# Expert blocks of 96 rows instead of 128, a shorter routing list, score products issued in pairs

## The reference

```
n = rmsnorm(x);  z = n @ w_in            # 1024 -> 3072: q, k, v, and B, C, h of the convolution
o = rmsnorm(diff_attention(q, k, v))     # 4 heads, two softmax maps each, relative-position bias
c = rmsnorm(B * causal_conv(C * h))      # width 3
h = x + concat(o, c) @ w_out
m = rmsnorm(h)
group = argmax(m @ router_group)         # 4 groups of 8 experts
top 2 of the group's 8 experts, gates from two softmaxes
y = h + sum over the token's 2 experts e of gate[e] * (silu(m @ w_gate[e]) * (m @ w_up[e])) @ w_down[e]
out = rmsnorm(y)
```

## Time and profile before

| what | value |
|---|---|
| median of three runs | 1072.74 us (1069.87 to 1073.26) |
| the profiled execution | 1070.95 us, its span 1069.1 us |
| TensorE busy | 916.2 us (86%) |
| VectorE busy | 577.2 us (54%) |
| ScalarE busy | 499.4 us (47%) |
| GpSimd busy | 442.3 us (41%) |
| moved over the span | 206.25 MB, mean 193 GB/s |

### The profile page before, as it was taken

The page is one execution under the profiler, slowest core; times in us unless marked ns, Lnnn a source line. Parts: engine busy times, 40 slices in busy tenths (PEclk is TensorE's granted clock), DMA queues, the critical chain, the costliest instruction groups (busy, mean ns, idle before and its releaser), DMA issues.

```text
span 1069.1 us, 14098 instructions
## 1 busy us (share of the span) xinstructions
PE 916.2 (86%) x4937; PEld 749.7 (70%) x4937; DVE 577.2 (54%) x1032; ACT 499.4 (47%) x830; POOL 442.3 (41%) x332
## 2 busy tenths in 40 slices
PE   4899999999999999958969997289999999999700
PEld 3799887888788778845757665178888887777500
DVE  4504532353325332767645137787777767767347
ACT  4423344334433434253312121558888877777412
POOL 1102322222332323223313120078999975565475
PEclk9999999999999999979979998589999999999955
DMA  8033223232121103270253521989999999998785
GB/s 263 18 93 101 80 80 94 88 99 80 41 62 30 51 28 103 86 236 1 83 168 119 177 84 64 360 311 376 410 412 406 413 405 399 402 397 329 280 283 204
DMA packets 92554, 206.25 MB, mean 193 GB/s; under 512 B 12767, under 2 KB 54303, under 8 KB 84294
## 3 DMA queue, kind: packets, MB, share of 16 engines
q1 hardware_dynamic: 79950, 168.13, 43.3%
q10 hardware_dynamic: 5528, 20.04, 4.8%
q0 software_dynamic: 7008, 17.18, 4.5%
HBM read 171.19 MB, written 42.34 MB: 200 GB/s over the span
## 4 chain that ended last, share of the span: by engine, by line
PE 66%; DVE 10%; DMA 9%; issue 5%; POOL 4%; ACT 4%; SPq 2%; ACTq 0%; POOLq 0%; DVEq 0%
PE pj L971 25%; PE pj L1854 11%; PE pj L1060 7%; DMA e_raw<-in_w_up 7%; PE pj L1900 6%; PE pj L1037 5%; PE pj L1022 3%; POOL f_y L2112 2%; PE tp L1829 2%; PE tp L1011 1%; DVE e_lo L1806 1%; DVE sc L1253 1%; DMA k_page<-in_cache_k 1%; PE pj L1452 1%; PE tp L994 1%
## 5 line engine op out<-in xcount | busy, mean ns | idle before, releaser
L971 PE MATMUL pj<-n_hi,w_hi 128*128 128x350 f32 (+1 forms) x576 | 200.3, 348 | 3.4 <-DVE n_lo L1291 3.4
L1806 POOL TENSOR_TENSOR e_lo<-e_raw,e_hid 128x2048 fp32r<-128x2048 f32 x32 | 167.6, 5237 | 72.8 <-ACT e_hid L1802 72.7
L971 PE MATMUL pj<-n_lo,w_hi 128*128 128x350 f32 (+1 forms) x576 | 188.4, 327 | 0.0
L971 PE MATMUL pj<-n_hi,w_lo 128*128 128x350 f32 (+1 forms) x576 | 187.5, 325 | 0.0
L1806 DVE TENSOR_TENSOR e_lo<-e_raw,e_hig 128x2048 fp32r<-128x2048 f32 x64 | 148.6, 2324 | 0.1
L669 POOL TENSOR_TENSOR w_lo<-w_raw,w_hi 128x1024 fp32r<-128x1024 f32 x21 | 50.1, 2388 | 204.5 <-ACT w_hi L744 204.5
L1802 ACT ACTIVATE e_hig<-e_raw 128x2048 fp32r<-128x2048 f32 x64 | 122.7, 1919 | 25.3 <-DMA e_raw<-in_w_up 18.7
L971 PEld LDWEIGHTS pj<-n_hi,w_hi 128*128 128x128 f32 x576 | 109.7, 190 | 32.3 <-issue 30.4
L1253 DVE CUSTOM_DVE_ANT_0 sc<-pj,strip 128x512 f32<-128x512 f32 (+5 forms) x120 | 61.6, 545 | 102.1 <-PE pj L1037 60.6
L971 PEld LDWEIGHTS pj<-n_lo,w_hi 128*128 128x128 f32 x576 | 110.0, 191 | 0.6
L971 PEld LDWEIGHTS pj<-n_hi,w_lo 128*128 128x128 f32 x576 | 109.8, 191 | 0.7 <-issue 0.6
(11 more groups left out here) (257 smaller groups left out, 1710.8 us busy)
## 6 DMA issues: line engine op xcount, KB each, us to landing
e_raw<-in_w_up SPq DMA_DIRECT2D x32, 1024.0 KB, 18.3
e_raw<-in_w_gate SPq DMA_DIRECT2D x32, 1024.0 KB, 20.4
e_raw<-in_w_down SPq DMA_DIRECT2D x32, 1024.0 KB, 21.9
expert_rows<-yo ACTq DMA_DIRECT2D x32, 512.0 KB, 8.2
w_raw<-in_w_in SPq DMA_DIRECT2D x24, 512.0 KB, 3.9
expert_rows<-logits SPq DMA_DIRECT2D x16, 512.0 KB, 5.1
wo_raw<-in_w_out SPq DMA_DIRECT2D x8, 512.0 KB, 5.0
k_page<-in_cache_k SPq DMA_DIRECT2D x16, 256.0 KB, 3.8
```

Source lines behind the costliest of these rows:

```text
L971: ins = pe.matmul(pj[g % 2][:, 0:tn], ws[w][:, P * k:P * (k + 1)], x[:, k, t0:t0 + tn], start=(m == 0), stop=(m == 23))
L1806: eng.tensor_tensor(e_lo[r][:, q, :], e_raw[r][:, q, :], e_hi(par, q).bitcast(F32), ALU.subtract).then_inc(s_lo[q], 1)
```

## The change

- Blocks have CB = 96 rows: transposes, stores, lists and one-hot tables shrink to 96; the products keep their 512 moving columns. Up to XB = 22 further blocks (rows beyond 96 of an expert) instead of 16.
- Score products wait for both banks and are issued together, with 12 instead of 6 filling matmuls between pieces.
- The weights of experts 0 and 1 are loaded in slot 51, behind the store of tile 7, in other buffers; those of experts 2 and 3 no longer wait for gathers. Expert 0 is rounded in slot 54.
- The top-2 search has fewer steps. The first list covers 32 blocks only, so place and token tables need neither overflow nor prefix sums; the placement products of tiles 0 to 6 (14) are issued before the last tiles' marks, those of tiles 7 and 8 (4) after.
- All the rest of the routing (`route_more`, 14 steps) runs on VectorE in the expert loop, with `pe_more` on TensorE in blocks 7, 9 and 11, and the two exponentials (`act_gates`) on ScalarE in block 1.
- The zeroing of the gather buffer is gone; it lies where finite rows lay before.
- GpSimd's difference of the down matrix is made in four parts of 512 columns.

From `dve_r` go the steps L1653 to L1694 after the placement (overflow, prefix sums, block index, one-hot tables over 48 blocks, list, addresses, gates); from `act_r` the zeroing and the exponentials; from `sp_m` the waits shown. The core of the diff, eight columns of indentation cut:

```diff
-MAXB = 48
-XB = MAXB - NE
+CB = 96
...
+                load_piece(sp, 0, q, 0, 0, 0)
+            sp.wait_ge(s_dm, MIXN[(NT - 1, 0)] + 1)
+            for q in (1, 0, 2):
+                load_piece(sp, 1, q, 1, 0, 1)
 def low_w(eng, n):
     eng.wait_ge(s_whi, n + 1)
...
+                high(act, 0, q, 0, 0)
 def act_conv_out(act, h):
     evacuated(act, chunk_of("GB", h, 2))
...
+        pe.wait_ge(s_sb, u)
     for c in range(2):
-        u = PIE[s] + 2 * p + c
-        if u >= 2:
-            pe.wait_ge(s_sb, u - 1)
         pe.matmul(pj[2 + c][0:M, 0:kn], qT[h % 2][DH * c:DH * (c + 1), P * i:P * i + M], kT[h % 2][DH * c:DH * (c + 1), k0:k0 + kn],
...
-                fill(ga, 6)
+                fill(ga, 12)
...
+            if i == NT - 1:
...
+            if i == NT - 1:
...
-        do(dve.scalar_tensor_tensor(tmp, tmp, -64.0, over_rows(iota32, T, n), ALU.mult, ALU.add))
-        do(dve.tensor_reduce(idx, tmp, AX.X, ALU.min))
-        do(dve.tensor_scalar(idx, idx, 64.0, None, ALU.add))
+        do(dve.tensor_tensor(tmp, tmp, over_rows(code, T, n), ALU.mult))
+        do(dve.tensor_reduce(v, tmp, AX.X, ALU.max))
...
-    do(dve.tensor_tensor(eq[:, t0:t1], over_rows(C("iotag"), T, NE), each(gs[:, 1, t0:t1], T, NE), ALU.is_equal))
-    do(dve.tensor_scalar(eq[:, t0:t1], eq[:, t0:t1], -1.0, BIG, ALU.add, ALU.mult))
-    do(dve.tensor_tensor(lem[:, t0:t1], eq[:, t0:t1], e, ALU.add))
+    dve.tensor_tensor(grp[:, 1, t0:t1], g, each(gs[:, 0, t0:t1], T, NG), ALU.subtract).then_inc(s_rx, 1)
+    do(dve.tensor_tensor(eq[:, t0:t1], over_rows(C("codeg"), T, NE), each(gs[:, 1, t0:t1], T, NE), ALU.not_equal))
+    do(dve.scalar_tensor_tensor(lem[:, t0:t1], eq[:, t0:t1], -BIG, e, ALU.mult, ALU.add))
...
+def tokens(dve, did, t0, t1):
+    T = t1 - t0
+    dve.wait_ge(s_step, did.n[0])
+    for c in range(2):
+        did(dve.tensor_tensor(block_tok[:, c, t0:t1], hot2[:, c, t0:t1], each(C("token1")[:, t0:t1], T, NE), ALU.mult))
...
-        did(dve.tensor_tensor(over2[:, c, t0:t1], each(rk[:, 0, c, t0:t1], T, 8), over_rows(C("over"), T, 8), ALU.is_ge))
-    dve.wait_ge(s_step, did.n[0])
-    do(dve.tensor_reduce(rk[:, 2, :, t0:t1], over2[:, :, t0:t1], AX.X, ALU.add))
-    do(dve.scalar_tensor_tensor(rk[:, 3, :, t0:t1], rk[:, 2, :, t0:t1], -float(P), rk[:, 0, :, t0:t1], ALU.mult, ALU.add))
-    for c in range(2):
-        dve.tensor_tensor(place_hot[:, c, t0:t1], over_rows(C("iota128"), T, P), each(rk[:, 3, c, t0:t1], T, P), ALU.is_equal).then_inc(s_ph, 1)
+        dve.tensor_tensor(place_hot[:, c, t0:t1], over_rows(C("iota128"), T, CB), each(rk[:, 0, c, t0:t1], T, CB), ALU.is_equal).then_inc(s_ph, 1)
...
+    route_rank(dve, did, TE, NT)
     route_place(dve, did, TE, NT)
...
+    do(dve.tensor_copy(cnt[:], rank_ps[:, NT, :]))
+    dve.wait_ge(s_pm, 1)
+    do(dve.tensor_scalar(slot_f[0:CB, :], pj[1][0:CB, 0:NE], 0.0, 4096.0, ALU.is_equal, ALU.mult))
+    do(dve.scalar_tensor_tensor(slot_f[0:CB, :], pj[1][0:CB, 0:NE], -1.0, slot_f[0:CB, :], ALU.add, ALU.add))
+    do(dve.tensor_copy(slot_tok[0:CB, 0:NE], slot_f[0:CB, :]))
+    dve.sem_inc(s_slots, 1)
...
+def route_more(dve, did, n):
...
-        do(dve.tensor_tensor(nx[(i + 1) % 2], nx[i % 2], nxs[:, i % 2, NE - d:2 * NE - d], ALU.add))
     upto, below = nxs[:, 1, NE:2 * NE], nxs[:, 1, NE - 1:2 * NE - 1]
-    for c in range(2):
-        did(dve.tensor_tensor(big2[:, c], hot2[:, c], over_rows(below, NT, NE), ALU.mult))
-    dve.wait_ge(s_step, did.n[0])
-    do(dve.tensor_reduce(rk[:, 1], big2[:], AX.X, ALU.add))
-    flat = [rk[:, i].rearrange("p a b -> p (a b)") for i in range(8)]
-    eif = ei[:].rearrange("p a b -> p (a b)")
-    do(dve.scalar_tensor_tensor(flat[4], flat[1], float(NE - 1), eif, ALU.add, ALU.subtract))
-    do(dve.tensor_tensor(flat[4], flat[4], flat[2], ALU.add))
-    do(dve.scalar_tensor_tensor(flat[4], flat[2], 1.0, flat[4], ALU.min, ALU.mult))
-    do(dve.tensor_tensor(flat[6], flat[4], eif, ALU.add))
-    for c in range(2):
-        do(dve.tensor_tensor(block_hot[:, c], over_rows(C("iota128")[:, 0:MAXB], NT, MAXB), each(rk[:, 6, c], NT, MAXB), ALU.is_equal))
-        dve.tensor_tensor(block_tok[:, c], block_hot[:, c], each(C("token1"), NT, MAXB), ALU.mult).then_inc(s_ph, 1)
-    do(dve.scalar_tensor_tensor(flat[7], flat[3], float(MAXB), flat[6], ALU.mult, ALU.add))
-    dve.wait_ge(s_pm, 1)
-    do(dve.tensor_scalar(slot_f[:], pj[1][:, 0:MAXB], 0.0, 4096.0, ALU.is_equal, ALU.mult))
-    do(dve.scalar_tensor_tensor(slot_f[:], pj[1][:, 0:MAXB], -1.0, slot_f[:], ALU.add, ALU.add))
-    did(dve.tensor_copy(slot_tok[:], slot_f[:]))
-    dve.wait_ge(s_step, did.n[0])
-    dve.sem_inc(s_slots, 1)
-    did(dve.tensor_copy(addr[:], flat[7]))
-    do(dve.tensor_tensor(xl[:], each(C("iotax"), XB, NE), over_rows(upto, XB, NE), ALU.is_ge))
-    do(dve.tensor_reduce(xlf[:, 0:XB], xl[:], AX.X, ALU.add))
-    do(dve.tensor_scalar(xlf[:, 0:XB], xlf[:, 0:XB], float(NE - 1), None, ALU.min))
-    do(dve.tensor_copy(xlf[:, XB:XB + 1], nxs[:, 1, 2 * NE - 1:2 * NE]))
-    did(dve.tensor_copy(xlist[:], xlf[:]))
-    dve.wait_ge(s_re, 4)
-    do(dve.tensor_reduce(gs[:, 3, :], grp[:, 2], AX.X, ALU.add))
-    do(dve.tensor_scalar(gs[:, 5, :], gs[:, 4, :], 1.0, None, ALU.add))
-    do(dve.tensor_tensor(gs[:, 3, :], gs[:, 3, :], gs[:, 5, :], ALU.mult))
-    do(dve.reciprocal(gate_w[:, 0, :], gs[:, 3, :]))
-    do(dve.tensor_tensor(gate_w[:, 1, :], gate_w[:, 0, :], gs[:, 4, :], ALU.mult))
-    dve.sem_inc(s_slots, 1)
+    flat = [rk[:, i].rearrange("p a b -> p (a b)") for i in range(7)]
+    evf = ev[:].rearrange("p a b -> p (a b)")
+    if n == 0:
+        did(dve.memset(nxs[:, :, 0:NE], 0.0))
+        do(dve.tensor_tensor(over_e[:], spread(cnt[:], [[1, NE], [0, OV]]), over_rows(C("over"), NE, OV), ALU.is_gt))
+        do(dve.tensor_reduce(nx[0], over_e[:], AX.X, ALU.add))
+    elif n == 1:
+        for i, d in enumerate((1, 2, 4, 8, 16)):
+            do(dve.tensor_tensor(nx[(i + 1) % 2], nx[i % 2], nxs[:, i % 2, NE - d:2 * NE - d], ALU.add))
+    elif n in (2, 3):
+        c = n - 2
+        do(dve.tensor_tensor(big_x[:], hot2[:, c], over_rows(below, NT, NE), ALU.mult))
+        do(dve.tensor_reduce(rk[:, 1, c], big_x[:], AX.X, ALU.add))
+    elif n == 4:
+        for c in range(2):
+            did(dve.tensor_tensor(over2[:, c], each(rk[:, 0, c], NT, OV), over_rows(C("over"), NT, OV), ALU.is_ge))
+        dve.wait_ge(s_step, did.n[0])
+        do(dve.tensor_reduce(rk[:, 2], over2[:], AX.X, ALU.add))
+        do(dve.scalar_tensor_tensor(flat[3], flat[2], -float(CB), flat[0], ALU.mult, ALU.add))
+        do(dve.scalar_tensor_tensor(flat[4], flat[1], float(NE - 1) - CODE, evf, ALU.add, ALU.add))
+        do(dve.tensor_tensor(flat[4], flat[4], flat[2], ALU.add))
+    elif n == 5:
+        do(dve.scalar_tensor_tensor(flat[4], flat[2], 1.0, flat[4], ALU.min, ALU.mult))
+        do(dve.scalar_tensor_tensor(flat[5], flat[4], CODE, evf, ALU.add, ALU.subtract))
+        for c in range(2):
+            do(dve.tensor_tensor(hot_x[:], over_rows(C("iota128")[:, NE:MAXB], NT, XB), each(rk[:, 5, c], NT, XB), ALU.is_equal))
+            do(dve.tensor_tensor(tok_x[:, c], hot_x[:], each(C("token1"), NT, XB), ALU.mult))
+    elif n in (6, 8, 10):
+        for j in (n - 6, n - 5):
+            c, t0 = j // 3, 3 * (j % 3)
+            if j >= 2:
+                dve.wait_ge(s_pm, j)
+            dve.tensor_tensor(place_x[:, j % 2], over_rows(C("iota128"), 3, CB), each(rk[:, 3, c, t0:t0 + 3], 3, CB), ALU.is_equal).then_inc(s_ph, 1)
+    elif n == 7:
+        do(dve.scalar_tensor_tensor(flat[6], flat[3], float(MAXB), flat[5], ALU.mult, ALU.add))
+        did(dve.tensor_copy(addr[:], flat[6]))
+    elif n == 9:
+        for b in range(2):
+            part = slice(XB // 2 * b, XB // 2 * (b + 1))
+            do(dve.tensor_tensor(xl[:], each(C("iota128")[:, part], XB // 2, NE), over_rows(upto, XB // 2, NE), ALU.is_ge))
+            do(dve.tensor_reduce(xlf[:, part], xl[:], AX.X, ALU.add))
+    elif n == 11:
+        do(dve.tensor_scalar(xlf[:, 0:XB], xlf[:, 0:XB], float(NE - 1), None, ALU.min))
+        do(dve.tensor_copy(xlf[:, XB:XB + 1], nxs[:, 1, 2 * NE - 1:2 * NE]))
+        did(dve.tensor_copy(xlist[:], xlf[:]))
+    elif n == 12:
+        dve.wait_ge(s_pm, 7)
+        do(dve.tensor_scalar(slot_x[0:CB, :], pj[2][0:CB, 0:XB], 0.0, 4096.0, ALU.is_equal, ALU.mult))
+        do(dve.scalar_tensor_tensor(slot_x[0:CB, :], pj[2][0:CB, 0:XB], -1.0, slot_x[0:CB, :], ALU.add, ALU.add))
+        did(dve.tensor_copy(slot_tok[0:CB, NE:MAXB], slot_x[0:CB, :]))
+    elif n == 13:
+        dve.wait_ge(s_re, 4)
+        do(dve.tensor_reduce(gs[:, 3, :], grp[:, 2], AX.X, ALU.add))
+        do(dve.tensor_scalar(gs[:, 5, :], gs[:, 4, :], 1.0, None, ALU.add))
+        do(dve.tensor_tensor(gs[:, 3, :], gs[:, 3, :], gs[:, 5, :], ALU.mult))
+        do(dve.reciprocal(gate_w[:, 0, :], gs[:, 3, :]))
+        do(dve.tensor_tensor(gate_w[:, 1, :], gate_w[:, 0, :], gs[:, 4, :], ALU.mult))
+        dve.sem_inc(s_slots, 1)
...
```

(49 more changed lines are left out.)

223 lines of the change are left out of this document (116 added, 107 removed).

## The result

The kernel after takes 1078.86 us (median, 1076.48 to 1080.60) against 1072.74 us: the ratio is 1.0067, 95% interval 1.0045 to 1.0089, so the change made the kernel slower by 0.7%, where 1049 us had been forecast. The profiled execution took 1080.1 us (span 1078.3).

The account below looks back on a forecast made before the run. TensorE was taken to bound attention, VectorE's serial sort the routing, and TensorE, then weight transfers, the expert loop. Gains of 5 + 9.5 + 8 - 0.5 + 0.6 = 22.6 us gave 1049 us, range 1040 to 1060.

Parts of the forecast that it names:

- Part 3: Expert loop: smaller blocks shorten it by 8 us, bounds 2 and 13.
- the quarters: Expert loop: GpSimd's difference in four parts takes 5.18 us, 0.6 more than one, costed at nothing given 4 us slack.
- the routing steps: Expert loop, blocks 2 to 13: 0.5 to 2.0 us each on VectorE, costed at nothing, as VectorE waits 1.89 us there.
- The period of 9.21 us: Expert loop: TensorE's time per block falls from 9.34 by 0.13 us, since transposes move 96 columns instead of 128.
- The transfers' period of 9.63 us: Late expert loop: stores smaller by 0.131 MB bring the transfers' time per block down from 9.96 us.
- The start: Last tile to first expert: first gate/up product at 692 instead of 701.2, 9.5 us gained with the earlier mix.
- The slots: Routing before the expert loop: slot list ready at 679 instead of cast at 690.79.
- the pairs: Attention: score products issued together gain 8 - 3 = 5 us, between 0 and 8; rival that they bring nothing, 0.11.
- The end: End loop over 22 instead of 16 possible further blocks is hidden; smaller overlaps, among them the last store, gain 0.6 us.
- the table loads in block 1: ScalarE in block 1: two loads of 1.28 us around the gates' exponentials, charged 0.5 us, up to 3.
- no further block: Expert loop: no expert exceeds 96 rows; the rival that one does costs some 30 us, 1079, chance 0.02.
- VectorE sets the period: Rival, expert loop: VectorE's differences wait for GpSimd's parts; slower than before needs above 9.98 us a block; chance 0.03.

Follow-up runs that it names:

- the shared version: Kernel after with routing steps first in the turn, GpSimd subtracting 1536 elements and VectorE 512, one test before the end loop: 1064.31 us, 0.9927.
- the zeros: Kernel after with GpSimd's four operations a block writing zeros in place of the down matrix's difference: 1059.20 us, 0.9874.
- the fourth round: Later side-by-side timing in which the kernel after, unchanged, was measured again: 1074.61 us, ratio 1.0022 to the kernel before (1072.77 us).

## Why the prediction was wrong

The forecast for the profiled span was 1046.5 us, and it was 1078.3: 31.8 us to account for.

- **The expert loop, 22.6 us of it.** Forecast 7.5 us shorter, measured 15.1 longer. The step that failed is in Part 3, and twice the same one: the quarters were costed at nothing because GpSimd had 4 us of slack, and the routing steps at nothing because VectorE waits 1.89 us behind the product with the gate. Both looked for idle time of the engine concerned. But while GpSimd's difference runs, an operation of VectorE with both inputs in SBUF doesn't, and the other way round; and VectorE's idle time lay under GpSimd's piece, just where the steps were put. In each block VectorE needs 2 x 2.28 us and GpSimd 4.6 in one piece, one after the other 9.2 of the 9.36 us of a block in which TensorE is never idle (blocks 15 to 30 of the shared version), and 5.0 in quarters, 9.6 in all. There was no room at all. With GpSimd's reading gone, 15.4 us go with it. Sharing that is an estimate, since the two costs aren't separate: taken out of the loop altogether, the steps give back 11.5 us of it, of which 3.0 had been charged (2.5 and 0.5); moved first in the turn they give 0.59% or 6.3 us (ratios 1.0022 and 0.9963, from two rounds); most of the rest is the quarters against VectorE's differences.
- **The rule of the Trainium skill** (SBUF — State Buffer, section Who interferes with whom) had been read as shortening VectorE's longest wait. The section says more: a VectorE instruction with two SBUF inputs contends with a GpSimd instruction that reads SBUF, not with one that only writes it. The runs show each clause: 4.25 us for a step behind a whole piece, 0.41 for the product with one input in PSUM, 0.17 beside the zeros. The prediction's own reading of a row for it, 805.23 behind 805.18, was luck: VectorE's instruction before it had just ended. A held operation shows by its length and not by a late start, and the row that does bear the rule out was beside it: GpSimd's piece from 799.69 takes 5.49 us, 0.92 more than the quickest, and VectorE's difference from 798.40 runs 0.99 us into it. No sum was drawn from that.

```profile
798.40 2.28 DVE L1806 TENSOR_TENSOR e_lo<-e_raw,e_hig 128x2048 fp32r<-128x2048 f32 x1
804.02 1.29 DVE L1842 TENSOR_TENSOR xT_lo<-tp,xT_hi 128x512 fp32r<-128x512 f32 x2 [0.43 <-ACT xT_hi L1837]
```

- **The period of 9.21 us.** TensorE alone, with nothing in its way, goes at 9.36 us (the same blocks). Fewer columns in the transposes brought nothing: from the start of the eight to the next product it is 0.81 us before (802.70 to 803.51) and 0.80 in the shared version. 31 blocks at 0.15 are 4.7 us, part of the 22.6.

```profile
803.51 0.48 PE L1854 MATMUL pj<-e_hig,xT_hi 128*128 128x512 f32 x1
...
906.25 1.02 PE L1902 MATMUL tp<-cst,xg 96*128 96x96 f32 x8
907.05 0.46 PE L1927 MATMUL pj<-e_hig,xT_hi 128*96 128x512 f32 x1
```

- **The transfers' period of 9.63 us.** Smaller stores did not shorten it: where a version with 96 rows waits for weights, its blocks take 10.0 to 10.3 us in the mean, and 10.03 before the change. In the kernel after this costs nothing, since it is slower anyway.
- **The start, 4.7 us.** The first SiLU is 9.8 us earlier and not 14.5. The slots (forecast 679, less the 5 of the pairs) and the issue of the weights came as worked out. Two terms are mis-sized. The pairs were put at 5 us and measure 2.6: the score products got 8 us shorter, as in the sum, but more than the 3 set against it came back in waits elsewhere. And the way from the slots to the first product is 2.4 us longer than forecast, because the differences that VectorE makes "under cover of the gather" hold up GpSimd's issue of the second gather, 2.94 us instead of 1.01. That is the contention of the loop once more.
- **The end, 4.5 us** (3.9 longer, forecast 0.6 shorter). The step: hidden, since SyncE and GpSimd wait for the last store anyway. That left out VectorE, which runs the same loop and makes the first final sum. At 0.53 us a turn it comes out about when the rows arrive, and in the fourth round the end is 65.5 us, 0.5 shorter than before, as forecast. The 4.5 us of the first profile are the 0.70 us stalls in VectorE's last turns, which no reading of the kernel before could show.
- **Right:** the table loads in block 1 (two of 1.28 us, at 700.96 and 704.62), no further block. What the loads cost the loop isn't separated. That transfers are no limit in the late blocks is no success: the blocks had become slower than the transfers. Of the rivals, *VectorE sets the period* came nearest: a mean of 10.01 us a block with 9.98 as its threshold. Its chance of 0.03 was too small, as its price was thought of as a sum of waits that needs 2.8 us more per block, and the slack for that had been read from busy times.

Not settled: why VectorE in some blocks gets in after a quarter and in others only after all four, and so how long a run of quarters holds it; and what the stalls at the end are.

The fastest whole version, 1062.1 us, keeps the change and has the steps first in the turn, 1536 elements on GpSimd and 512 on VectorE, the order forced by a wait, and one test ahead of the end loop.

## What to carry to other kernels

Before work is put into an engine's idle time, ask what else runs then: idle time of VectorE under a GpSimd operation that reads SBUF is no room for an operation with two SBUF inputs, though it is for one that reads PSUM. Add up the time of the two engines' SBUF operations in a period as if they were one engine, and if it comes near the period, fix their order; a piece cut in parts gives more chances to be in the way. And a loop over work that doesn't exist has a price on every engine that runs it (here 0.53 us a turn on VectorE), also on the one that nobody is watching; it is hidden only as long as that engine has to wait anyway.

## What the runs showed of the hardware

- An operation on 128 x 18 elements took 0.17 us alone, 0.9 to 1.2 behind a GpSimd quarter and 4.25 behind a whole piece: its recorded time includes the wait, and no idle time appears before it. The only sign is the same line with two durations.
- Four zero fills of 128 x 512 on GpSimd (0.53 us each) did not stretch VectorE's operations with two inputs in SBUF (2281 ns for its differences, 0.17 us for a step).
- The issue of a gather on GpSimd takes 0.97 us, and 2.85 where a difference of VectorE runs (909.25 in the kernel after). With zeros in the loop no gather meets a difference, and each takes 0.96; ahead of the loop one does there too, and takes 2.94.
- A cast of 128 x 18, with a single input, was held too: 0.18 us in the kernel before, 1.20 beside the quarters, and 0.44 beside the zeros, where it ended with the last zero fill, so that here writing was enough to hold it. A reduction of 128 x 180, with a single input, took 0.34 in both.
- An empty turn of a loop with a test inside took VectorE 0.53 us. 22 of them kept it idle for 16.4 to 17.1 us in three profiles, where single register instructions stalled for 0.70 us, and for 12.1 us in four later ones that end with no wait.
- Eight transposes with 96 moving columns kept TensorE for 0.80 us up to the next product, with 128 for 0.81.
